# Feed-forward gate and up as 2x2 blocks with seven products instead of eight

## The chip, the cores and the metric

The kernel runs on one core of one Trainium2 chip. The metric is the device time of one execution in microseconds. Three runs of the kernel before took 2939.01, 2939.33 and 2942.37 us; the median is 2939.33 us.

## The reference, cut to what matters

Two transformer-like blocks are computed for 1024 tokens of width 1024, in float32. The change touches the end of the first block, its feed-forward part:

```
h2 = ada_norm(x, norm2_g, sh2, sc2)
gt, up = jnp.split(h2 @ w_gu, 2, axis=-1)          # w_gu: 1024 x 5632, D_FF = 2816
x = x + g2 * ((jax.nn.silu(gt) * up) @ w_down)     # w_down: 2816 x 1024
```

D_FF is 22 tiles of 128 features. A second block (a state-space mixer, then a stick-breaking attention) follows. Its modulation vectors come from three matrices `ada_w_2` and `kv_ada_w_2` times an activated vector `c_2`; that product has nothing to do with the feed-forward and is computed beside it.

## The kernel before, in words

Everything is kept transposed: 128 features on the partitions, 1024 tokens along the row. Every float32 factor is split into a high part, which ScalarE copies to the type fp32r, and a low part, which VectorE subtracts (raw minus high). A product is then three matmuls: high by high, high by low, low by high. A matmul has a 128x128 weight and 512 tokens. `hH` and `hL` are the high and low parts of the eight tiles of h2.

A gate or up tile is one unit: 8 input tiles, 2 token halves and 3 products, 48 matmuls, into one of two PSUM units `PU`. A panel of weights (`w_raw`, 512 KB; `split` on ScalarE and on VectorE) holds one unit's weights. SyncE loads the panels in the order of use. `w_raw`, `w_hi_t` and `w_lo_t` have two buffers each.

Tile 0 is special: its gate and up run on the un-normalised tiles while the norm is still being computed, and are scaled afterwards. VectorE meanwhile writes the normalised tiles (`row_scaled` writes a tile `n_h`, `row_low` writes its low part). Tile 1's gate and up (`paired`, L1158) start when the tiles come, one tile after another.

Then ten rounds of a loop (`ffn_body`) follow, each for two tiles: gate, up, gate, then `down` of the two tiles before, then up. `down` takes two gated tiles as input: 2 panels of 4 units with 12 matmuls each; VectorE adds every unit to the residual `xT` (L3283). The gated tiles never leave the chip. ScalarE computes silu of the gate (L2372), VectorE multiplies by up (L3274), and both split the product (L2377, L3278).

In the first eight rounds a job runs beside: eight slabs of 128x1024 of the modulation matrices, loaded by GpSimd (L975, L977), multiplied and accumulated by VectorE (L2765), transposed and reduced (L2754, L2755) and turned into a column by four narrow matmuls on TensorE (`ada_columns`, L1204), which wait for the reduction (`ada_acc_s`). A slab is loaded when the slab two before it is used (`ada_used`).

Each engine executes its own list in the order written; waits are semaphores.

Of the kernel before, what the change touches and what calls it, by code (L numbers as in the profile page):

```python
# [166 lines left out]
M_UNIT0 = len(WIN_UNITS) + HEAD_UNITS + TT // 2 + KD + 4 * (FT // 2) + KD * (FT // 2)  # L167
# [22 lines left out]
OUT_PANEL0 = len(WIN_UNITS) + KD + 6 * (FT // 2) + 14 * NG + 2 * KD + 2 * SB_PAIRS  # L190
# [36 lines left out]
RAW_SCALED = 5  # L227
W_OUT_ORDER = (0, 1, 2, 3, 4, 6, 7, 5)
# [3 lines left out]
def two_blocks(nc, a, out):  # L232
# [8 lines left out]
    scr_g = nc.dram_tensor("mixer_inverse_rows", (KD, TT, 2, P), F32, kind="Internal").ap()  # L241
    scr_y = [nc.dram_tensor(f"kept_group_{n}", (4, P, T), F32, kind="Internal").ap() for n in ("high", "low")]
    ctx = ExitStack()
    with ctx:
# [105 lines left out]
        f_silu = at("f_silu", A, [P, 2, T])  # L350
        f_prod = at("f_prod", A + 2048, [P, 2, T])
        f_hi = at("f_hi", A + 4096, [P, 2, T], F32R)
        f_lo = at("f_lo", A + 6144, [P, 2, T], F32R)
# [6 lines left out]
        dt_p = at("dt_p", A + 13312, [P, KD, NH])  # L360
# [109 lines left out]
        ada0_landed = [sem(f"ada0_landed{n}") for n in range(4)]  # L470
# [12 lines left out]
        x_landed = [sem(f"x_pair_landed{t}") for t in range(TT // 2)]  # L483
# [22 lines left out]
        nv_tr = sem("na_values_transposed")  # L506
        nv_tok = sem("na_values_token_major")
        na_s = sem("na_scores_done")
        na_l = sem("na_logits_ready")
        na_e = sem("na_exp_done")  # L510
        na_tr = sem("na_probs_transposed")
        na_ev = [sem("na_probs_evacuated_even"), sem("na_probs_evacuated_odd")]
        na_evx = sem("na_last_keys_evacuated")
        na_pv = sem("na_values_summed")
        na_o = sem("na_output_written")
        wu_landed = sem("w_uq_w_ukv_landed")
        q_rot = sem("mla_queries_rotated")
        kr_landed = sem("mla_rotary_keys_placed")
# [3 lines left out]
        mla_m = sem("mla_minimum_ready")  # L522
# [81 lines left out]

        block = ctx.enter_context(nc.Block())
# [3 lines left out]
        def _(sp):  # L609
# [69 lines left out]
            def gate_up(i, t, up):  # L679
                panel(w_gu[:, :, bass.ds((2 * i + t) * P + up * DFF, P)], KD, P)  # L680
# [13 lines left out]
            for t, up in ((0, 0), (0, 1), (1, 0), (1, 1)):  # L694
                if (t, up) == (1, 0):
                    token_rows(0)
                    sp.wait_ge(c_inv, INVERSES + 1)
                gate_up(0, t, up)
            with sp.Fori(0, FT // 2 - 1) as i:
                pc.enter(i, 6)  # L700
                gate_up(i + 1, 0, 0)
                gate_up(i + 1, 0, 1)
                gate_up(i + 1, 1, 0)
                down(i)
                gate_up(i + 1, 1, 1)
            pc.leave(FT // 2 - 1)
            down(FT // 2 - 1)


# [144 lines left out]
        def _(g):  # L854
# [94 lines left out]
            ada2 = a["ada_w_2"].rearrange("l (k p) c -> p l k c", p=P)  # L949
            kva = a["kv_ada_w_2"].rearrange("(k p) c -> p k c", p=P)  # L950
# [21 lines left out]
            with counted(g, 8, [(pc, KD), (slab, KD)]) as i:  # L972
                for k in range(KD):
                    sl = slab_free()
                    g.dma_start(ada_w[:, sl, 0:768].rearrange("p (l c) -> p l c", l=2), ada2[:, :, k, bass.ds(3 * P * i, 3 * P)])\  # L975
                        .then_inc(ada_landed[sl], 16)
                    g.dma_start(ada_w[:, sl, 768:1024], kva[:, k, bass.ds(2 * P * i, 2 * P)]).then_inc(ada_landed[sl], 16)  # L977
                    slab_next()
# [67 lines left out]
        def _(pe):  # L1046
# [21 lines left out]
            def feat_unit(wp, c0, width, kt, aH, aL, panel_last=True, mid=None, ready=None, late=None):  # L1068
# [3 lines left out]
                for half in range(2):  # L1072
                    cols = slice(half * 512, (half + 1) * 512)
                    for k in range(kt):
# [3 lines left out]
                        whi = w_hi_t[:, wp, w0:w0 + width]  # L1078
                        wlo = w_lo_t[:, wp, w0:w0 + width]
# [116 lines left out]
            def ada_columns():  # L1196

                n = job.next()
                s = (job.n - 1) % 2
                pe.wait_ge(ada_acc_s, n)  # L1200
                if job.n > 2:
                    pe.wait_ge(ada_mod, n - 2)
                for q in range(4):
                    last = mm(PM[32 * q:32 * q + 32, 2 + s, 0:KD], fold[:, 0:32], ada_red[:, s, q::4], start=True, stop=True)  # L1204
                last.then_inc(ada_col, 1)
# [363 lines left out]
            paired(hr())  # L1569
            hr.next(KD)  # L1570
            fa = Tally()

            def down():
                pe.wait_ge(f_act, fa.next(2))
                for c in range(2):
                    wp = panel_ready()
                    for u in range(4):
                        feat_unit(wp, u * P, P, 2, f_hi, f_lo, panel_last=u == 3)

            def last_down():  # L1580
                both = fa.next(2)
                wp, u0 = panel_ready(), unit_open()
                p1, n1 = uc.at(1)
                pair = ((u0, 0), (p1, P))

                def part(up, c0, k, half, w, side, first=False, final=False):
                    w0 = k * 512 + c0
                    return mm(PU[:, up, half, :], w[:, wp, w0:w0 + P], side[:, k, half * 512:(half + 1) * 512],
                              start=first, stop=final)

# [2177 lines left out]
```

## Time and profile before

| | |
|---|---|
| median of three runs | 2939.33 us |
| profiled execution, device time | 2943.62 us |
| its span | 2941.8 us |
| TensorE busy | 2870.7 us, 98% |
| VectorE busy | 1748.7 us, 59% |
| ScalarE busy | 1039.3 us, 35% |
| GpSimd busy | 446.6 us, 15% |
| mean granted TensorE clock | 0.991 |
| feed-forward, tile 0's gate to the last down unit | about 739 to 1465 us of the span |

Busy time of TensorE is counted from overlapping matmuls: one of 512 columns is shown as 0.39 us long, and the next starts 0.227 us after it. The distance between starts, not the length, says what a matmul costs.

### The profile page before, as it was taken

The page shows a single profiled execution, that of the slowest core. Times are in us where ns is not written, and L with a number is a line of the kernel's source. Part 1 is how long each engine was busy: PE and PEld are TensorE (multiplying, and loading weights), DVE is VectorE, ACT ScalarE, POOL GpSimd, SP SyncE. Part 2 cuts the span into 40 slices and gives each one's busy share as a digit, 9 for nine tenths or more (in the row PEclk, how much of TensorE's full clock was granted, in tenths as well). Part 3 has the DMA queues.
Part 4 walks back from the last instruction along what each step waited for, and adds up shares of the span by engine and source line. Part 5 has one row for each costly group of instructions (what it writes and reads, how often), then busy time and mean ns, then how long its engine had stood idle before and what let it go on. Part 6 is the DMA issues. An engine that isn't in the chain of part 4 may idle for free.

```text
span 2941.8 us, 40297 instructions
## 1 busy us (share of the span) xinstructions
PE 2870.7 (98%) x16452; PEld 2271.7 (77%) x16452; DVE 1748.7 (59%) x1932; ACT 1039.3 (35%) x1343; POOL 446.6 (15%) x508
## 2 busy tenths in 40 slices
PE   6998999999999999999999999999999999999999
PEld 5886667778888888888877888888778887777677
DVE  6557638763755555543467848668768345455463
ACT  4124445652411111111235424334434114444462
POOL 3012010001211111110102103021212002223240
PEclk8999999999999999999989999999999999999999
DMA  7454011101333333331115233243531321212121
GB/s 244 144 166 108 6 30 31 30 23 43 103 120 108 100 107 110 111 93 50 43 45 152 72 93 108 79 131 103 179 111 51 108 91 60 72 37 70 39 87 58
DMA packets 248122, 258.66 MB, mean 88 GB/s; under 512 B 14431, under 2 KB 208656, under 8 KB 247968
## 3 DMA queue, kind: packets, MB, share of 16 engines
q1 hardware_dynamic: 223280, 179.70, 19.9%
q0 software_dynamic: 19008, 59.19, 6.9%
q10 hardware_dynamic: 5680, 17.58, 1.5%
q8 instruction: 113, 1.85, 0.3%
q14 instruction: 41, 0.34, 0.0%
HBM read 223.41 MB, written 30.65 MB: 86 GB/s over the span
## 4 chain that ended last, share of the span: by engine, by line
PE 89%; DVE 4%; ACT 3%; issue 1%; DMA 1%; SPq 1%; POOL 0%; ACTq 0%; DVEq 0%; POOLq 0%
PE PU L1080 18%; PE PU L1082 17%; PE PU L1081 17%; PE PU L1858 2%; PE PM L1882 2%; PE PM L1870 2%; PE PM L1902 2%; PE PU L1096 2%; PE PU L1097 2%; PE PU L1098 2%; PE PU L1469 2%; PE PM L1904 2%; PE PM L1903 2%; PE PU L1391 2%; ACT m_p L2311 1%
## 5 line engine op out<-in xcount | busy, mean ns | idle before, releaser
L1080 PE MATMUL PU<-hH,w_hi_t 128*128 128x512 f32 x1792 | 706.1, 394 | 0.8 <-DVE w_lo_t L2727 0.6
L1082 PE MATMUL PU<-hH,w_lo_t 128*128 128x512 f32 x1792 | 698.4, 390 | 0.0
L1081 PE MATMUL PU<-hL,w_hi_t 128*128 128x512 f32 x1792 | 697.7, 389 | 0.0
L1082 PEld LDWEIGHTS PU<-hH,w_lo_t 128*128 128x128 f32 x1792 | 335.1, 187 | 72.4
L1080 PEld LDWEIGHTS PU<-hH,w_hi_t 128*128 128x128 f32 x1792 | 335.3, 187 | 71.5 <-issue 1.7
L1081 PEld LDWEIGHTS PU<-hL,w_hi_t 128*128 128x128 f32 x1792 | 335.4, 187 | 68.9
L2727 DVE TENSOR_TENSOR w_lo_t<-w_raw,w_hi_t 128x1024 fp32r<-128x1024 f32 x180 | 234.7, 1304 | 216.2 <-ACT w_hi_t L2016 208.4
L2016 ACT ACTIVATE w_hi_t<-w_raw 128x1024 fp32r<-128x1024 f32 x166 | 174.2, 1049 | 410.5 <-PE PU L1082 327.9
L3283 DVE SCALAR_TENSOR_TENSOR xT<-PU,mod,xT 128x1024 f32<-128x1024 f32 x120 | 153.8, 1282 | 158.5 <-PE PU L1082 158.5
L3627 DVE TENSOR_TENSOR_SCAN s_keep<-s_keep,zero 128x128 f32<-128x128 f32 (+7 forms) x128 | 182.0, 1423 | 76.3 <-POOL s_keep L1035 76.3
L1035 POOL TENSOR_SCALAR_AFFINE_SELECT s_keep<-s_keep 128x128 f32<-128x128 f32 x128 | 93.9, 740 | 467.0 <-ACT s_keep L2613 466.6
L1080 PE MATMUL PU<-f_hi,w_hi_t 128*128 128x512 f32 x344 | 133.9, 389 | 1.3 <-DVE xT L3283 1.3
L1082 PE MATMUL PU<-f_hi,w_lo_t 128*128 128x512 f32 x344 | 133.8, 389 | 0.0
L1081 PE MATMUL PU<-f_lo,w_hi_t 128*128 128x512 f32 x344 | 133.8, 389 | 0.0
L2620 ACT ACTIVATE s_at<-PM 128x128 f32<-128x128 f32 (+7 forms) x128 | 83.5, 652 | 141.7 <-PE PM L1870 141.2
L1096 PE MATMUL PU<-hH,w_hi_t 128*128 128x512 f32 x304 | 123.2, 405 | 6.3 <-DVE hL L2805 5.8
L1097 PE MATMUL PU<-hL,w_hi_t 128*128 128x512 f32 x304 | 120.5, 396 | 0.0
L1098 PE MATMUL PU<-hH,w_lo_t 128*128 128x512 f32 x304 | 120.2, 395 | 0.0
L998 POOL TENSOR_TENSOR xw<-xt,wend 128x512 f32<-128x512 f32 x28 | 38.0, 1357 | 499.3 <-PE PU L1082 195.7
L975 POOL DMA_DIRECT2D ada_w<-in_ada_w_dram x64 | 45.6, 713 | 433.7 <-DVE ada_acc L2765 305.0
L2765 DVE SCALAR_TENSOR_TENSOR ada_acc<-ada_w,cact,ada_acc 128x1024 f32<-128x1024 f32 x84 | 107.5, 1280 | 2.2
L1902 PE MATMUL PM<-hH,w_hi_t 128*128 128x512 f32 x224 | 98.7, 440 | 0.0
(518 smaller groups left out, 5007.5 us busy)
## 6 DMA issues: line engine op xcount, KB each, us to landing
ada_w<-in_ada_w_dram POOLq DMA_DIRECT2D x64, 384.0 KB, 4.0
w_raw<-in_w_gu_dram SPq DMA_DIRECT2D x44, 512.0 KB, 3.8
w_raw<-in_m_in_w_dram SPq DMA_DIRECT2D x40, 512.0 KB, 3.9
ada_w<-in_w_ada_dram POOLq DMA_DIRECT2D x32, 512.0 KB, 4.8
seg<-decay_sums SPq DMA_DIRECT2D x32, 512.0 KB, 4.1
w_raw<-in_w_down_dram SPq DMA_DIRECT2D x22, 512.0 KB, 3.3
w_raw<-in_w_in_dram SPq DMA_DIRECT2D x17, 512.0 KB, 3.9
ada_w<-in_w_ada_dram SPq DMA_DIRECT2D x16, 512.0 KB, 14.5
```

The source lines that it names most:

```text
L1080: mm(PU[0:width, up, half, :], whi, aH[:, k, cols], start=k == 0, stop=False)
L1081: mm(PU[0:width, up, half, :], whi, aL[:, k, cols], start=False, stop=False)
L1082: last = mm(PU[0:width, up, half, :], wlo, aH[:, k, cols], start=False, stop=k == kt - 1)
L1096: mm(PU[0:width, up, half, :], whi, hH[:, k, cols], start=first, stop=False)
L1097: mm(PU[0:width, up, half, :], whi, hL[:, k, cols], start=False, stop=False)
L1098: return mm(PU[0:width, up, half, :], wlo, hH[:, k, cols], start=False, stop=final)
L1902: mm(PM[:, 3, :], whi, hH[:, j, cols], start=j == 0, stop=False)
L2016: af(w_hi_t[:, p, 0:w], w_raw[:, p, 0:w], ACT.Copy).then_inc(w_hi[p], 1)
L2727: V.tensor_tensor(w_lo_t[:, p, 0:w], w_raw[:, p, 0:w], w_hi_t[:, p, 0:w].bitcast(F32), ALU.subtract)\
L2765: ins = V.scalar_tensor_tensor(acc, w, cv[:, k:k + 1], acc, ALU.mult, ALU.add)
L3283: free(V.scalar_tensor_tensor(xT[:, t, :], unit_ps(p), m(g, t), xT[:, t, :], ALU.mult, ALU.add))
L3627: V.tensor_tensor_scan(keep[:, ::-1], keep[:, ::-1], zero[:, :].broadcast_to([P, w]), 1.0, ALU.mult, ALU.max).then_inc(s_a, 1)
```

## The change

Tiles 2 to 21 (20 tiles) are computed as a 2x2 by 2x2 block product. The weight's four blocks are gate or up, by even or odd input tiles (each 4 tiles of 128x128). The input's four blocks are even or odd input tiles, by first or second 512 tokens. Eight block products become seven, each over 4 tiles: 7 x 4 x 3 = 84 matmuls for a tile's gate and up. A block product is a `phase`. The sums of input blocks are formed once by GpSimd from `n_h` (`t_formed`), and split by ScalarE and VectorE into `t_hi`, `t_lo` and the second half of the even tiles of `hH`, `hL`. The sums of weight blocks are formed for every tile by GpSimd (`weight_sums`, 4 operations of 128x512). Each phase's weight is split anew (`phase_high` on ScalarE, `phase_low` on VectorE, 128x512, four buffers). The results are combined in PSUM and by five VectorE additions.

The feed-forward becomes two passes. The first writes all gated tiles to DRAM (`scr_f`), the second loads them back and runs all eleven `down` pairs one after another, with the same 1056 matmuls as before. The modulation job is cut into 16 half jobs, one for each of the tiles 2 to 17, of 8 slabs of 128x512, now loaded by SyncE in two transfers each; `ada_columns` runs at the end of each of the 16 tiles.

SyncE, one body for four tiles (`rows_body`; `gate_up_rows` loads 2 x 512 KB, the weights of the tile after next):

```diff
+            def ada_slabs(i, r, ks):
+                c, l = 2 * i + r // 2, r % 2
+                for k in ks:
+                    if k == 1:
+                        sp.wait_ge(ada_acc_s, ADA_JOBS + 4 * i + r)
+                    else:
+                        sp.wait_ge(ada_used, slab(-1))
+                    dst = ada_half[:, k % 2, :]
+                    sp.dma_start(dst[:, 0:384], ada2[:, l, k, bass.ds(3 * P * c, 3 * P)]).then_inc(half_landed[k % 2], 16)
+                    sp.dma_start(dst[:, 384:512], kva[:, k, bass.ds(2 * P * c + l * P, P)]).then_inc(half_landed[k % 2], 16)
+                    slab.next()
+            def rows_body(i, jobs, rows=range(4)):
+                for r in range(4):
+                    if jobs:
+                        ada_slabs(i, r, range(4))
+                    if r in rows:
+                        sp.wait_ge(gu_low, GU_LOW + 28 * i + 7 * r + 7)
+                        gate_up_rows(r, 4 * i + r + 4)
+                    if jobs:
+                        ada_slabs(i, r, range(4, KD))
...
+            gate_up_rows(0, 2)
+            sp.wait_ge(unit_free[1], D_UNIT0 // 2)
+            sp.dma_start(scr_f[1, :, :], f_second[:, :]).then_inc(f_stored, 16)
+            sp.wait_ge(f_stored, F_STORED + 32)
+            gate_up_rows(1, 3)
```

TensorE:

```diff
+            def phase(i, r, q):
+                slot = phase_slot(7 * r + q)
+                pe.wait_ge(gu_low, GU_LOW + 28 * i + 7 * r + q + 1)
...
+                for k in range(4):
...
+                    mm(bank, gu_hi[slot][:, k, :], high, start=first, stop=False, skip_group_check=check)
+                    mm(bank, gu_hi[slot][:, k, :], low, start=False, stop=False, skip_group_check=check)
+                    last = mm(bank, gu_lo[slot][:, k, :], high, start=False, stop=k == 3, skip_group_check=check)
+                last.then_inc(gu_done, 1)
+            def phases_body(i, jobs):
+                for r in range(4):
+                    for q in range(7):
+                        phase(i, r, q)
+                    if jobs:
+                        ada_columns(4, half_columns)
+            with counted(pe, 4, [(job, 4)]) as i:
+                phases_body(i, 1)
+            phases_body(4, 0)
```

VectorE, for one tile r (`tt` is an addition; `done` counts the tile's finished phases):

```diff
+                    phase_low(i, r, 4)
+                    half_slabs((0, 1))
+                    ve.wait_ge(gu_done, done + 2)
+                    tt(mid, PM[:, 1, :], mid, ALU.add).then_inc(gu_added, 1)
+                    phase_low(i, r, 5)
+                    ve.wait_ge(gu_done, done + 3)
+                    ve.wait_ge(f_kept, F_KEPT + 64 * i + 16 * r)
+                    tt(f2, PM[:, 2, :], mid, ALU.add).then_inc(gu_added, 1)
+                    phase_low(i, r, 6)
+                    half_slabs((2, 3))
+                    ve.wait_ge(gu_done, done + 4)
+                    tt(f2, PM[:, 3, :], f2, ALU.add).then_inc(gu_added, 1)
...
+                        phase_low(i, r + 1, 0)
+                        half_slabs((4, 5))
+                        phase_low(i, r + 1, 1)
+                        half_slabs((6, 7))
...
+                    ve.wait_ge(gu_done, done + 6)
+                    tt(f1, PM[:, 2, :], mid, ALU.add).then_inc(gu_added, 1)
+                        phase_low(i, r + 1, 2)
+                    ve.wait_ge(gu_done, done + 7)
+                    tt(mid, PM[:, 3, :], mid, ALU.add).then_inc(gu_added, 1)
+                        phase_low(i, r + 1, 3)
```

GpSimd, and the waits that its sums put into VectorE's norm loop; and VectorE in the second pass:

```diff
+            for k in range(4):
+                g.wait_ge(h_tmp, KD + 2 * k + 2)
...   # four subtractions of 128x512, each counted by t_formed
+            def halves_gated(i, r):   # two multiplications of 128x512, then the store
...
+                g.dma_start(scr_f[bass.ds(4 * i + r + 2, 1), :, :].rearrange("o p t -> (o p) t"), f_out[:, :]).then_inc(f_kept, 16)
...
+                    if k:
+                        ve.wait_ge(t_formed, T_FORMED + (4 * (k // 2) + 2 if k % 2 else 2 * k))
                     row_scaled(k + 1, coef[:, 1, :], n_rs[:, :])
...
+            def down_body(b):
+                down_units("g2", range(4))
+                tile_low(2 * b)
+                tile_low(2 * b + 1)
+                down_units("g2", range(4, 8))
```

`phase_high` on ScalarE waits until the phase four before it is done (`gu_done`). `gate_up_rows(0, 2)` waits for all sixteen input sums. At the end of the first pass ScalarE waits for the last store (`f_kept`) before it splits the second down panel.

## Rows read from the trace of the kernel before

**Rows 1.** The page: engines, and the chain that ended last.
```profile
PE 2870.7 (98%) x16452; PEld 2271.7 (77%) x16452; DVE 1748.7 (59%) x1932; ACT 1039.3 (35%) x1343; POOL 446.6 (15%) x508
PE 89%; DVE 4%; ACT 3%; issue 1%; DMA 1%; SPq 1%; POOL 0%; ACTq 0%; DVEq 0%; POOLq 0%
```

**Rows 2.** Windows: busy PE, PEld, DVE, ACT, POOL; clock; DMA share; GB/s.
```profile
881.00:944.00 63.00, 63.00 (x286) 51.91 (x285) 34.04 (x31) 10.08 (x10) 8.46 (x14) 1.00 0.35 105
```

**Rows 3.** Timeline of TensorE: start, length, line, tiles.
```profile
1000.24 0.39 PE L1080 MATMUL PU<-hH,w_hi_t 128*128 128x512 f32 x1
...
1005.68 0.39 PE L1080 MATMUL PU<-hH,w_hi_t 128*128 128x512 f32 x1
```

**Rows 4.** Timeline of VectorE in the loop.
```profile
897.60 1.28 DVE L3283 SCALAR_TENSOR_TENSOR xT<-PU,mod,xT 128x1024 f32<-128x1024 f32 x1 [0.30 <-PE PU L1082]
900.32 1.28 DVE L3283 SCALAR_TENSOR_TENSOR xT<-PU,mod,xT 128x1024 f32<-128x1024 f32 x1 [1.44 <-PE PU L1082]
...
911.86 1.25 DVE L2754 STREAM_TRANSPOSE ada_acc<-ada_acc 128x1024 f32<-128x1024 f32 x1
913.14 1.22 DVE L2755 TENSOR_REDUCE ada_red<-ada_acc 128x32 f32<-128x1024 f32 x1
...
977.56 1.25 DVE L2754 STREAM_TRANSPOSE ada_acc<-ada_acc 128x1024 f32<-128x1024 f32 x1
```

**Rows 5.** Groups by shape, VectorE and ScalarE: count, busy, mean ns.
```profile
L3442 DVE TENSOR_TENSOR xt<-xt,xl 128x512 f32<-128x512 f32 x28 | 19.4, 692 | 1.0
L3429 DVE TENSOR_TENSOR state<-state,PM 128x512 f32<-128x512 f32 x24 | 16.5, 687 | 0.8
L3158 DVE SCALAR_TENSOR_TENSOR y_att<-y_att,vec,PM 128x512 f32<-128x512 f32 x2 | 1.5, 747 | 3.9 <-PE PM L1519 3.9
L2298 ACT ACTIVATE m_pt<-PM 128x512 f32<-128x512 f32 x64 | 34.8, 594 | 81.3 <-PE PM L1483 81.2
```

**Rows 6.** Tile w_raw, its issues (ns min/median/max); transfers in 1334:1342.
```profile
L628 SPq DMA_DIRECT2D w_raw<-in_w_gu_dram x5: 372/373/373, 1335.6 to 1400.9; - x5
w_raw<-in_w_gu_dram SPq DMA_DIRECT2D x1, 512.0 KB, 3.7
q1 hardware_dynamic: 1040, 0.52, 22.3%
```

**Rows 7.** Timeline of GpSimd and VectorE, alone and side by side.
```profile
719.77 2.40 POOL L960 TENSOR_TENSOR n_acc<-n_acc,n_sq 128x1024 f32<-128x1024 f32 x1 [8.48 <-ACT n_sq L2044]
741.53 3.34 POOL L960 TENSOR_TENSOR n_acc<-n_acc,n_sq 128x1024 f32<-128x1024 f32 x1 [1.87 <-ACT n_sq L2044]
730.68 6.72 DVE L2820 SCALAR_TENSOR_TENSOR hL<-xT,coef,hH 128x1024 fp32r<-128x1024 f32 x5
741.34 5.81 DVE L2820 SCALAR_TENSOR_TENSOR hL<-xT,coef,hH 128x1024 fp32r<-128x1024 f32 x3
```

**Rows 8.** TensorE around a pause: windows of 1 us, and its timeline.
```profile
424.00:425.00 1.00, 1.00 (x14) 0.77 0.07 16
425.00:426.00 1.00, 1.00 (x8) 0.50 0.00 0
420.38 1.84 PE L1507 MATMUL PM<-blk,u_sq 128*128 128x2 f32 x16
423.64 0.50 PE L1461 MATMUL PU<-kr_hi,w_lo_t 32*128 32x512 f32 x4 [1.41 <-ACT m_p L2311]
425.55 0.63 PE L1469 MATMUL PU<-k_hi,qk_lo 64*128 64x512 f32 x2
```

**Rows 9.** Timeline, VectorE's norm loop and tile 1's results.
```profile
755.24 1.29 DVE L2805 SCALAR_TENSOR_TENSOR hL<-n_h,mod,hH 128x1024 fp32r<-128x1024 f32 x1
773.75 2.59 DVE L2805 SCALAR_TENSOR_TENSOR hL<-n_h,mod,hH 128x1024 fp32r<-128x1024 f32 x2
785.66 1.23 DVE L3274 TENSOR_TENSOR f_prod<-PU,f_silu 128x1024 f32<-128x1024 f32 x1 [0.85 <-PE PU L1098]
```

**Rows 10.** Timeline of TensorE at the end of the feed-forward.
```profile
1448.75 0.50 PE L1080 MATMUL PU<-f_hi,w_hi_t 128*128 128x512 f32 x1 [1.28 <-DVE xT L3283]
```

More of the change, by code:

```diff
@@ L710, in _ @@
+            with sp.Fori(0, 4) as x:
+                pc.enter(x, 4)
+                for b in range(2):
+                    down_body(2 * x + 1 + b, b)
+                pc.leave(4)
+            down_body(9, 0)
+            down(10)
             m_in = a["m_in_w_2"].rearrange("o (k p) c -> p (o k) c", p=P)
@@ L971, in _ @@
                     g.dma_start(small[32 * q:32 * q + NH, c:c + 1], a[name].rearrange("o h -> h o")).then_inc(rp_landed, 16)
[L972 to L978, printed above, removed]
+            even, odd = n_h[:, 0, :], n_h[:, 1, :]
@@ L2365, in _ @@
-            up = Tally(1)
-            def gate(t, ahead=False):
-                if not ahead:
-                    split()
-                p = unit()
-                free(af(f_silu[:, t, :], unit_ps(p), ACT.Silu))
-            def high(t, upu):
-                act.wait_ge(unit_free[upu[0]], upu[1] + 1)
-                up.next()
-                af(f_hi[:, t, :], f_prod[:, t, :], ACT.Copy).then_inc(f_hi_s, 1)
+            af(f_first[:, 0, :], f_first[:, 0, :], ACT.Silu, bias=small[:, 44:45]).then_inc(raw_gate, 1)
@@ new lines, in _ @@
+            for n in range(2):
+                for k in range(4):
+                    token_sum_high(n, k)
+            act.wait_ge(raw_scaled, 4)
+            phase_high(0, 0, 0)
+            token_sum_high(3, 0)
+            token_sum_high(3, 1)
+            act.wait_ge(f_stored, F_STORED + 16)
+            phase_high(0, 0, 1)
+            token_sum_high(3, 2)
+            p = unit()
+            free(af(f_second[:, :], unit_ps(p), ACT.Silu))
+            token_sum_high(3, 3)
+            used.next(KD - 1)
@@ L2379, in passed @@
+            with act.Fori(0, 4) as i:
+                highs_body(i)
+            highs_body(4, last=True)
+            for n in (2, 3):
+                tile_high(n, 1)
             def passed(units):
@@ L3298, in ffn_body @@
+            with counted(ve, 4, [(slab, 4 * KD), (job, 4), (reduced, 4), (ch, 4)]) as i:
+                lows_body(i, 1)
+            lows_body(4, 0, last=True)
+            tile_low(2)
+            tile_low(3)
+            ve.wait_ge(gu_done, GU_DONE + 7 * F_PAIRS)
+            down_units("g2", range(4))
+            down_units("g2", range(4, 8))
+            def down_body(b):
                 down_units("g2", range(4))
+                tile_low(2 * b)
+                tile_low(2 * b + 1)
                 down_units("g2", range(4, 8))
-                low(0)
@@ L3301, in ffn_body @@
-                up(1, todo[6:8])
-                low(1)
-                if jobs:
-                    ada_finish([(48 + 3 * i, 128 + 3 * i, 3), (72 + 3 * i, 152 + 3 * i, 3), (96 + 2 * i, 176 + 2 * i, 2)])
-                for c in (pc, uc, fh, job, slab, ch):
-                    c.leave(times)
-            low(0)
-            gate(ahead=True)
-            up(1)
-            low(1)
-            with ve.Fori(0, 8) as i:
-                ffn_body(i, 8, 1)
-            with ve.Fori(0, FT // 2 - 9) as i:
-                ffn_body(i, FT // 2 - 9, 0)
+            with counted(ve, 4, [(pc, 4), (uc, 16), (fh, 4)]):
+                down_body(0)
+                down_body(1)
```

476 lines of the change are left out of this document (313 added, 163 removed).

## The prediction

> **What bounds the kernel now.** I read the page first: TensorE is busy for 98% of the span and holds 89% of the chain that ended last [rows 1]. The window of one round of the feed-forward loop shows the same locally: TensorE busy for 63.00 of 63 us at full clock, VectorE for 34.04, GpSimd for 8.46, DMA share 0.35 [rows 2]. The busy sum can't price a matmul, because they overlap. In the timeline 24 matmuls start between 1000.24 and 1005.68 [rows 3], so one of 512 columns costs 0.227 us. A round has 4 x 48 + 8 x 12 = 288 matmuls, 65.3 us; two transposes of the job one round apart lie 65.7 us apart [rows 4]. The 0.4 us left are the narrow `ada_columns`. So TensorE alone sets the loop, and nothing else waits on its path.
>
> **What the change removes.** A tile's gate and up go from 96 to 84 matmuls, 21.8 to 19.0 us; a phase is 12 matmuls, 2.72 us. With 20 tiles that is 54.4 us. The `ada_columns` run 16 times instead of 8, 3.4 us more. If TensorE stayed the bound, 51 us would be gained. The 1056 `down` matmuls stay.
>
> **What it adds to a tile with a job (16 of the 20).** VectorE: 7 lows at 0.69 (two SBUF inputs), 5 additions from PSUM at 0.69, 8 half slabs at 0.75, a transpose and a reduction at about 0.7 each (half of 1.25 and 1.22 plus a start-up part) [rows 4, 5]: 15.6 us of 19.5. GpSimd: 6 operations of 128x512; one of 1024 takes 2.40 alone [rows 7], so about 1.2 each, and a store's issue: 8 us. ScalarE: 7 highs, a copy and two silus at 0.6 [rows 5], 6 us. DMA: 1 MB of weights, 2 MB of slabs, 0.5 MB stored. A 512 KB panel used 0.223 of 8 us [rows 6], 1.8 us of all engines, so 12 us. Every engine has room for its sum. So the order has to be walked, because TensorE ends each such tile with `ada_columns`, which waits for the reduction of this same tile's job.
>
> I count from the start of the tile's first phase. The third phase ends at 8.2 (3 x 2.72). Only then may ScalarE make the high part of the seventh phase (four buffers), and VectorE has the addition of the third phase before its low part: 0.7 and 0.7, with a little delay by GpSimd 10.0. SyncE has waited for just this low part, with the slabs 4 to 7 queued behind the wait. It issues the 2 x 512 KB of weights at 10.1. One panel lands 3.7 us after its issue [rows 6], the second 1.8 later: 15.6. Slab 4 (256 KB, 0.9 of data) stands behind them: 16.5. No row of before shows a small transfer behind two panels; the ends are 13.7 (issued 0.8 later, since an issue takes 0.37 [rows 6], landing 2.8, no queue) and 16.5, and I take the upper, since both lie on one queue that is full for those 3.6 us. Slab 4 is used by 17.3. Only that lets SyncE issue slab 6, which lands 2.8 later (3.7 less half the data), 20.2 with the hand-overs. Slabs 6 and 7 take VectorE to 21.7, transpose and reduction to 23.1, the columns to 23.6. TensorE finished its seven phases at 19.0 and stands idle for 4.1 us.
>
> The Trainium skill bears on the choice between the two ends (DMA: Bandwidth & Descriptors, Queues, rings and completion order): SyncE's transfers share one row of rings, and on each DMA engine descriptors are consumed in ring order. By that rule slab 4 waits for both panels and the tile takes 23.6 us; without it 20.8. No row here shows it.
>
> The pause has a second price. After 1.84 us of two-column matmuls and 1.41 us idle the granted clock fell to 0.50, and 512-column matmuls grew to 0.63 us [rows 8], for about 3 us. That is at most 1.6 us lost, part of it in the pause itself or behind the third phase, where it is covered. Between 0 and 1.6 I take 0.6. A tile with a job: 24.2 us against 21.97 before (half of 65.7 less 21.76 of `down`). 16 x 2.2 = +35.7 us.
>
> The other four tiles have no slabs. VectorE needs 8.3 of 19.0 us there and each low part is ready two phases early; 4 x (19.04 - 21.76) = -10.9.
>
> **Contention.** GpSimd and VectorE slow each other: `hL` takes 6.72 / 5 = 1.34 us alone, but three take 5.81 while GpSimd's addition runs, and that one grows from 2.40 to 3.34 [rows 7]. A 1024 operation on GpSimd costs VectorE up to 1.8 us, a 512 one 0.9; six make 5.4 at worst. Most fall where VectorE waits anyway; 0.3 us stands in the 10.0 above, up to 2 in the upper bound.
>
> **The start.** Four subtractions per pair of tiles, 4.8 us alone, now stand between `n_h` pairs: with one `row_scaled` (1.28) 6.1 us a pair, 8 with contention, against 5.1 before. The loop ran from 755.2 to 776.3 and tile 1's units ended at 785.6, without waiting for it [rows 9]; they had about 2 us of slack at the fourth tile. So tile 1 is late by 0 to 4 us. The first weight rows are loaded only after the last sum (781 to 787), take 5.5 to land and 1.4 to split: the first phase starts 2 to 8 us late. In its first tile SyncE stores tile 1, waits for that (about 3 us) and loads the next rows before any slab: the reduction comes 3 to 12 us later than in the steady walk. Together 5 to 20; I take +12.
>
> **Middle and second pass.** After the last phase: addition, silu, product, store and its landing, about 7 us, then the split of the second down panel. VectorE has that split ahead of its first evacuation, so the third unit waits: +4 (0 to 6). In each later pair two low parts and a split stand between evacuations 4 and 5: 10.9 + 1.3 + 3 x 1.2 + 1.3 = 17.1, while unit 7 wants its PSUM at 16.3 (units 2.72 us apart [rows 4]); overlapping starts take some back: 0.5 x 10 = +5 (0 to 8). The wait of 1.28 before the last `down` goes [rows 10]: -1.3.
>
> **Sum.** 35.7 - 10.9 + 12 + 4 + 5 - 1.3 = +44.5 us. The profiled execution took 2943.6 (span 2941.8 and 1.8 around it), so 2988 on its own time; the median is 4.3 lower, so 2984.
>
> **The rivals.**
> TensorE stays the bound (faster). If the reduction comes within 19.0 us, `ada_columns` finds it ready, and the tile costs 19.46: 16 x (19.46 - 21.97) = -40.2; -10.9; start +6, middle +4, second pass +5, -1.3: -37, 2902 us. For it: every engine has 20% to spare, and in the job before the reduction lay far ahead. It decides at the low part of the seventh phase plus 9 us; against it are the two serial landings with a panel pair in front of them.
> The slabs don't queue behind the panels. Slab 4 is there at 13.7, and all behind it is 2.8 us earlier: tile 20.8, 16 x -1.17 = -18.7; -10.9, start +8, +7.7 for the rest: -14, 2925 us. For it: the data are 0.9 us and the engines many. From a tile of 21.7 us on it is no gain.
> The pause feeds itself (slower still). The half clock hits the first phases in full, +1.6, and contention delays the seventh low part by 1.3: tile 26.5, 16 x 4.5 = +72; -10.9, start +18, rest +12: +91, 3030 us. For it are rows 7 and 8; against it, that a clock back at full inside 3 us leaves most of it covered.
>
> **How the numbers follow.** My walk 0.58, TensorE bound 0.14, no queue 0.14, feeding pause 0.14. The likeliest gives 2984 us; its own range is 2955 to 3012 (tile of 23 to 25.2, start 5 to 20). The range for 8 in 10 leaves out TensorE bound and the far part of the feeding pause: 2922 to 3020. A change of 0.2%, 6 us, is about what a measurement of this kernel can tell from none. Faster: 0.14 + 0.10 (most of no queue) = 0.24. Same: 0.05 (the edge of no queue and of my walk). Slower: 0.71.
>
> **What would show it.** In the profile after, two `ada_columns` of neighbouring tiles lie about 24 us apart in tiles 2 to 17 and 19 in the last four. In the first 16 TensorE waits about 4 us for VectorE's reduction, once a tile, and the clock shows 0.50 right after. The transfers of slab 4 land 6 us after the panel pair is issued. The second pass has waits of under 1 us for an evacuation. What would make me wrong: `ada_columns` without a wait before it, slabs landing in 3 us with panels in flight, or waits in front of the phases themselves, which the walk says have at least 5 us in hand.

## The result, and the profile after

The changed kernel took 3065.54 us (median of four runs, 3061.1 to 3070.56), the kernel before 2940.85 us beside it. The ratio is 1.0421, with a 95% interval of 1.0408 to 1.0434. It is slower, as forecast, but by 124.7 us where I forecast 45, and outside my range of 2922 to 3020. The profiled execution took 3061.1 us, the lowest of the four. Its span is 3059.5 us, 117.7 more than before, and the account below is of those 117.7.

First the page after: engines, and the chain that ended last. TensorE has less work than before, but its share of the chain fell from 89% [rows 1] to 74%, and a wait for slabs of the job (`ada_half`) stands in it.

```profile
PE 2865.9 (94%) x16276; PEld 2255.6 (74%) x16276; DVE 1928.4 (63%) x2217; ACT 1109.3 (36%) x1499; POOL 592.1 (19%) x536
PE 74%; DVE 9%; DMA 5%; issue 4%; ACT 4%; SPq 2%; POOL 1%; ACTq 0%; DVEq 0%; POOLq 0%
```

The windows show where: the fifteen tiles with a job behind the first (845 to 1249), the four without, and the second pass. Columns as in [rows 2]: the stretch, its length, busy PE, PEld, DVE, ACT, POOL, granted clock, DMA share, GB/s.

```profile
845.00:1249.00 404.00, 322.98 (x1372) 260.12 (x1370) 264.31 (x360) 90.47 (x150) 146.10 (x105) 0.88 0.45 136
1249.00:1329.00 80.00, 78.59 (x344) 64.57 (x344) 40.32 (x53) 24.55 (x39) 34.25 (x25) 0.97 0.28 92
1329.00:1583.00 254.00, 244.78 (x1056) 198.47 (x1056) 161.19 (x137) 51.20 (x50) 14.76 (x7) 0.99 0.25 87
```

In the first stretch TensorE is idle for a fifth of the time and its clock is 0.88, against 63.00 of 63 and 1.00 in [rows 2]. A tile takes 27.0 us there (the first and the last of sixteen reductions start at 843.20 and 1248.37, 15 tiles). No engine but TensorE is over 66% busy. The list of waits names one wait for all of it: line, what it waited for, us in total, times, longest.

```profile
PE PU L1357 <- DVE ada_red L2954: 87.3, 16, 7.1
```

One tile in detail, from TensorE's timeline. The columns wait for the reduction, as forecast, for 5 us. The first phase behind them starts its matmuls 0.427 us apart instead of 0.227 [rows 3]; it takes 5.3 us (1060.38 to 1065.67) instead of 2.72.

```profile
1060.16 0.29 PE L1357 MATMUL PU<-ada_red,fold 128*32 128x4 f32 x8 [4.99 <-DVE ada_red L2954]
1060.38 0.80 PE L1744 MATMUL PM<-hH,gu_hi 128*128 128x512 f32 x1
1060.98 0.63 PE L1745 MATMUL PM<-hL,gu_hi 128*128 128x512 f32 x1
1061.40 0.63 PE L1746 MATMUL PM<-hH,gu_lo 128*128 128x512 f32 x1
...
1065.67 0.41 PE L1744 MATMUL PM<-t_hi,gu_hi 128*128 128x512 f32 x1
```

Windows of 1 us, TensorE alone (busy, clock, DMA share, GB/s), show why: the clock is at 0.50, the lower level of 1.2 GHz, from 1059 to 1065.65. TensorE had been idle since about 1055.2.

```profile
1058.00:1059.00 1.00, 0.00 (x0) 0.94 0.43 115
1059.00:1060.00 1.00, 0.00 (x0) 0.50 0.48 147
...
1064.00:1065.00 1.00, 1.00 (x4) 0.50 0.00 0
1065.00:1066.00 1.00, 1.00 (x5) 0.65 0.12 49
```

The job's chain in the same tile: VectorE's timeline (the seventh low part, slabs 4 and 5, 6, 7, the reduction), then SyncE's (the panel pair, slab 4, slab 6).

```profile
1072.51 0.68 DVE L3486 TENSOR_TENSOR gu_lo<-gu_sum,gu_hi 128x512 fp32r<-128x512 f32 x1
...
1080.18 1.54 DVE L2964 SCALAR_TENSOR_TENSOR ada_half_acc<-ada_half,cact,ada_half_acc 128x512 f32<-128x512 f32 x2 [3.42 <-DMA ada_half<-in_kv_ada_w_dram]
...
1083.74 0.75 DVE L2964 SCALAR_TENSOR_TENSOR ada_half_acc<-ada_half,cact,ada_half_acc 128x512 f32<-128x512 f32 x1 [1.41 <-DMA ada_half<-in_kv_ada_w_dram]
1084.99 0.75 DVE L2964 SCALAR_TENSOR_TENSOR ada_half_acc<-ada_half,cact,ada_half_acc 128x512 f32<-128x512 f32 x1 [0.50 <-DMA ada_half<-in_kv_ada_w_dram]
...
1086.52 0.69 DVE L2954 TENSOR_REDUCE ada_red<-ada_half 128x16 f32<-128x512 f32 x1
```

```profile
1073.37 1.01 SPq L749 DMA_DIRECT2D gu_rows<-in_w_gu_dram  x2
1074.63 0.75 SPq L764 DMA_DIRECT2D ada_half<-in_ada_w_dram  x1
...
1081.10 0.33 SPq L764 DMA_DIRECT2D ada_half<-in_ada_w_dram  x1
```

Counted from the first phase at 1060.38, with the forecast in brackets: the panels are issued at 13.0 (10.1), slab 4 is used from 19.8 (landed at 16.5), slab 6 from 23.4 (20.2), the reduction ends at 26.8 (23.1). The order of events is that of the walk in the prediction. Of the 3.7 us that it is late, 2.9 are there when the panels are issued, and 2.6 of these are the slow first phase.

The start, from VectorE's and GpSimd's timelines. Beside GpSimd's subtractions VectorE's operations on 128x1024 take 2.29 instead of 1.29 us, and GpSimd's on 128x512 take 2.24 instead of 1.31: both take 1.7 to 1.8 times as long.

```profile
754.42 1.29 DVE L3005 SCALAR_TENSOR_TENSOR hL<-n_h,mod,hH 128x1024 fp32r<-128x1024 f32 x1
...
762.85 2.29 DVE L3005 SCALAR_TENSOR_TENSOR hL<-n_h,mod,hH 128x1024 fp32r<-128x1024 f32 x1
```

```profile
758.04 1.31 POOL L1086 TENSOR_TENSOR t_raw<-n_h 128x512 f32<-128x512 f32 x1
...
766.60 2.24 POOL L1086 TENSOR_TENSOR t_raw<-n_h 128x512 f32<-128x512 f32 x1 [2.55 <-DVE n_h L3001]
```

The loop over the normalised tiles takes 39.2 us (751.90 to 791.1), against 23.6 before (752.7 to 776.3 [rows 9]). TensorE's first phase starts at 806.69:

```profile
806.69 0.79 PE L1744 MATMUL PM<-hH,gu_hi 128*128 128x512 f32 x1 [7.83 <-DVE gu_lo L3486]
```

The second pass, from VectorE's timeline: two low parts and a split stand before an evacuation, and a pair of gated tiles is 22.59 us from the next (1369.06 to 1391.65) instead of 8 x 2.72 = 21.76 [rows 4].

```profile
1369.06 2.35 DVE L3510 TENSOR_TENSOR f_lo<-f_raw,f_hi 128x1024 fp32r<-128x1024 f32 x2
1371.33 1.22 DVE L2926 TENSOR_TENSOR w_lo_t<-w_raw,w_hi_t 128x1024 fp32r<-128x1024 f32 x1
1372.46 2.47 DVE L3461 SCALAR_TENSOR_TENSOR xT<-PU,mod,xT 128x1024 f32<-128x1024 f32 x2
...
1391.65 2.35 DVE L3510 TENSOR_TENSOR f_lo<-f_raw,f_hi 128x1024 fp32r<-128x1024 f32 x2
```

The account of the 117.7 us beside that of the prediction:

| part | forecast | measured | how measured |
|---|---|---|---|
| 16 tiles with a job | +35.7 | +80.6 | 16 x (27.0 - 21.97) |
| 4 tiles without | -10.9 | -7.2 | 1249.4 to 1329.2, less 4 x 21.76 |
| start | +12 | +32.2 | first phase 806.7, not 784.8 (785.6 [rows 9] less 0.8): 21.9; first tile 37.3, not 27.0: 10.3 |
| middle and second pass | +9 | +14.4 | 1329.2 to 1583.0, less 11 x 21.76 |
| wait before the last `down` | -1.3 | -1.3 | gone |
| loop starts earlier | 0 | -0.8 | 751.9, not 752.7 |
| sum | +44.5 | +117.9 | |

### The profile page after: what moved, and what is told of

It reads as the page before. It is cut to its first block, busy times and chain, and to the rows that moved or that the text cites. A ratio compares the mean times of both kernels' runs of the same rounds, so it can differ in the third digit from the quotient of the medians.

```text
span 3059.5 us, 41804 instructions
## 1 busy us (share of the span) xinstructions
PE 2865.9 (94%) x16276; PEld 2255.6 (74%) x16276; DVE 1928.4 (63%) x2217; ACT 1109.3 (36%) x1499; POOL 592.1 (19%) x536
## 4 chain that ended last, share of the span: by engine, by line
PE 74%; DVE 9%; DMA 5%; issue 4%; ACT 4%; SPq 2%; POOL 1%; ACTq 0%; DVEq 0%; POOLq 0%
PE PU L1232 12%; PE PU L1234 11%; PE PU L1233 11%; DMA ada_half<-in_kv_ada_w_dram 4%; PE PU L1998 2%; PE PM L2022 2%; PE PM L2010 2%; PE PM L2042 2%; PE PM L1744 2%; PE PM L2044 2%; PE PM L2043 2%; PE PU L1622 2%; PE PU L1248 2%; PE PM L1745 2%; PE PM L1746 2%
## 5 line engine op out<-in xcount | busy, mean ns | idle before, releaser
L1232 PE MATMUL PU<-hH,w_hi_t 128*128 128x512 f32 (+1 forms) x1152 | 455.9, 396 | 0.7 <-DVE w_lo_t L2926 0.6
L1234 PE MATMUL PU<-hH,w_lo_t 128*128 128x512 f32 (+1 forms) x1152 | 449.2, 390 | 0.0
L1233 PE MATMUL PU<-hL,w_hi_t 128*128 128x512 f32 (+1 forms) x1152 | 448.7, 389 | 0.0
L1234 PEld LDWEIGHTS PU<-hH,w_lo_t 128*128 128x128 f32 (+1 forms) x1152 | 214.9, 187 | 47.2
L1232 PEld LDWEIGHTS PU<-hH,w_hi_t 128*128 128x128 f32 (+1 forms) x1152 | 215.2, 187 | 46.4 <-issue 1.5
L1233 PEld LDWEIGHTS PU<-hL,w_hi_t 128*128 128x128 f32 (+1 forms) x1152 | 215.3, 187 | 44.0
L1744 PE MATMUL PM<-hH,gu_hi 128*128 128x512 f32 x320 | 142.0, 444 | 14.4 <-DVE gu_lo L3486 7.8
L1248 PE MATMUL PU<-hH,w_hi_t 128*128 128x512 f32 x304 | 125.1, 411 | 15.8 <-DVE hL L3005 8.4
L1745 PE MATMUL PM<-hL,gu_hi 128*128 128x512 f32 x320 | 137.8, 431 | 0.0
L1249 PE MATMUL PU<-hL,w_hi_t 128*128 128x512 f32 x304 | 121.7, 400 | 0.0
```

The lines of the kernel that those rows point to most:

```text
L1232: mm(PU[0:width, up, half, :], whi, aH[:, k, cols], start=k == 0, stop=False)
L1233: mm(PU[0:width, up, half, :], whi, aL[:, k, cols], start=False, stop=False)
L1234: last = mm(PU[0:width, up, half, :], wlo, aH[:, k, cols], start=False, stop=k == kt - 1)
L1248: mm(PU[0:width, up, half, :], whi, hH[:, k, cols], start=first, stop=False)
L1249: mm(PU[0:width, up, half, :], whi, hL[:, k, cols], start=False, stop=False)
L1744: mm(bank, gu_hi[slot][:, k, :], high, start=first, stop=False, skip_group_check=check)
```

## The experiments

The kernels are all built from the changed one ("after", 3065.5 us). A tile means the mean distance of the sixteen reductions.

**The slabs first.** The queue behind the panels is taken away. SyncE loads all eight half slabs of a tile before it waits for the seventh low part:

```diff
                     if jobs:
-                        ada_slabs(i, r, range(4))
+                        ada_slabs(i, r, range(KD))
                     if r in rows:
                         sp.wait_ge(gu_low, GU_LOW + 28 * i + 7 * r + 7)
                         gate_up_rows(r, 4 * i + r + 4)
-                    if jobs:
-                        ada_slabs(i, r, range(4, KD))
```

> The load order of SyncE alone is changed: all eight half slabs of a tile are issued before SyncE waits for the seventh low part and loads the next pair of weight panels. After, a tile with a job takes 27.0 us; slab 4 lands about 7 us after the panel pair's issue, and the reduction ends 15.9 us behind the third phase. Theory A (the two serial slab landings behind the panel pair set the tile): slab 4 no longer waits for the seventh low part or for the panels, the reduction comes 4 to 6 us earlier, TensorE's pause shrinks from 5 us to 0 to 1.5, and with it the time at half clock: tile 20.5 to 22.5 us, 16 x (-4.5 to -6.5) = -72 to -104 us, 2960 to 2995 us. Theory B (VectorE's slab work and its contention with GpSimd set the reduction, the landing is hidden behind them): the reduction moves by under 1.5 us, tile 25.5 to 27 us, 3040 to 3066 us. Theory C (panels now late behind the slabs): the waits move to the first phase of the next tile, tile above 24 us with TensorE waiting for a low part at the head of a tile, 3015 us or more.

Measured: 3009.22 us, 56 less than after, ratio 1.0229 to before (1.0212 to 1.0246); tile 23.7 us. That is between the theories. VectorE's timeline of this kernel (slabs 5, 6 and 7, the reduction), and SyncE's issues of the same three slabs:

```profile
950.70 0.75 DVE L2962 SCALAR_TENSOR_TENSOR ada_half_acc<-ada_half,cact,ada_half_acc 128x512 f32<-128x512 f32 x1 [0.91 <-DMA ada_half<-in_kv_ada_w_dram]
952.58 0.75 DVE L2962 SCALAR_TENSOR_TENSOR ada_half_acc<-ada_half,cact,ada_half_acc 128x512 f32<-128x512 f32 x1 [0.53 <-DMA ada_half<-in_kv_ada_w_dram]
954.39 0.75 DVE L2962 SCALAR_TENSOR_TENSOR ada_half_acc<-ada_half,cact,ada_half_acc 128x512 f32<-128x512 f32 x1 [1.05 <-DMA ada_half<-in_kv_ada_w_dram]
...
955.92 0.69 DVE L2952 TENSOR_REDUCE ada_red<-ada_half 128x16 f32<-128x512 f32 x1
```

```profile
948.04 0.33 SPq L764 DMA_DIRECT2D ada_half<-in_ada_w_dram  x1
...
949.95 0.33 SPq L764 DMA_DIRECT2D ada_half<-in_ada_w_dram  x1
...
951.61 0.33 SPq L764 DMA_DIRECT2D ada_half<-in_ada_w_dram  x1
```

From issue to use a slab takes 2.6 to 2.8 us with no panel ahead of it. In after slab 4 took 5.55 (1074.63 to 1080.18). The difference, 2.9 us, is what the 1 MB of panels ahead of it costs per tile, and the tile fell by 3.3. The Trainium skill (DMA: Bandwidth & Descriptors, Queues, rings and completion order) says that on each DMA engine descriptors are consumed in ring order, and these two numbers agree with it. They don't tell an order in the queue from panels and slab merely sharing the DMA engines; no run here separates the two. I had expected more because I overlooked that slabs 2 to 7 still stand behind the seventh low part in VectorE's own order, and then come one every 1.85 us, the turn-round of two buffers.

**The columns later.** The consumer is moved: `ada_columns` and VectorE's copy of them go behind the second phase of the next tile.

```diff
                     for q in range(7):
                         phase(i, r, q)
-                    if jobs:
-                        ada_columns(4, half_columns)
+                        if q == 1 and r in tiles:
+                            ada_columns(4, half_columns)
```

> Only the place of the consumer is changed: TensorE runs the four small column products of a tile's job behind the second phase of the next tile (VectorE's copy of them moves with it), loads and slab work stay in their order. If the 7.6 us by which a tile with a job exceeds its 84 matmuls and its columns (27.0 against 19.45) are all a wait for the reduction plus the half clock behind this wait, then 5.4 us of slack take the wait away whole, the clock stays up and the tile falls to 19.5 to 21.0 us: 16 x (-6 to -7.5) = -96 to -120, 2945 to 2970 us. If the job's chain itself is longer than a tile (the slabs and the low parts on VectorE and SyncE take over 21 us per tile whatever the place of the columns), the waits come back at the phases: tile 22 to 25 us, 2985 to 3035 us, with TensorE waiting for a low part.

Measured: 3024.82 us, ratio 1.0284 (1.0267 to 1.0301), tile 24.6 us. The second case. Two phases of slack took away only 2.4 us. VectorE's timeline (reduction, an addition, the low part of the next tile's third phase) and TensorE's show it:

```profile
1015.96 0.69 DVE L2955 TENSOR_REDUCE ada_red<-ada_half 128x16 f32<-128x512 f32 x1
1016.56 0.68 DVE L3560 TENSOR_TENSOR f_out<-PM,gu_mid 128x512 f32<-128x512 f32 x1
1017.16 0.68 DVE L3487 TENSOR_TENSOR gu_lo<-gu_rows,gu_hi 128x512 fp32r<-128x512 f32 x1
```

```profile
1016.77 0.25 PE L1357 MATMUL PU<-ada_red,fold 128*32 128x4 f32 x8 [2.10 <-DVE ada_red L2955]
...
1017.97 0.49 PE L1744 MATMUL PM<-t_hi,gu_hi 128*128 128x512 f32 x1 [0.95 <-DVE gu_lo L3487]
```

The third phase waits as well. So the tile is set by a ring, a chain of waits that closes on itself: the reduction stands ahead of the third phase's low part in VectorE's list; the third phase ahead of the seventh low part; this ahead of the panels; these ahead of slab 4; and slab 4 ahead of the next reduction.

**The pause filled.** This aims at the clock alone: 18 matmuls whose result is thrown away stand where TensorE was idle.

```diff
                     if jobs:
+                        for _ in range(18):
+                            mm(PU[:, 0, 1, :], hH[:, 1, 0:P], hH[:, 1, 0:512], start=True, stop=True)
                         ada_columns(4, half_columns)
```

> 18 matmuls of 128x512 whose product nobody reads (4.1 us at full clock) are put before the column products of each tile with a job, where TensorE stands idle for 5 us; nothing else is changed. They take nothing from the chain that ends in the reduction. If the half clock in the next tile's first phase (5.3 us instead of 2.72) is a cost of the pause and on the path, the clock stays at or near full and the tile falls from 27.0 to 24.3 to 24.9 us: -34 to -43 us, 3022 to 3032 us, and what remains is the walk's 23.6 us plus about 1. Rival, as the prediction had it: the half clock is mostly covered, the tile falls by 0.6 or less (3056 to 3066 us); or the extra matmuls run late and push the columns: 3066 us or more.

Measured: 3053.18 us, 12 less, ratio 1.0379 (1.0362 to 1.0396), tile 26.4 us on average. Neither expectation holds for the mean. Where the clock stayed at 1.00 a tile is 25.4 to 25.9 us; the others are 26.7 to 28.1. Windows of single tiles (columns as above):

```profile
898.00:926.00 28.00, 26.00 (x110) 20.99 (x110) 17.76 (x25) 6.03 (x10) 9.71 (x7) 0.89 0.45 133
1057.00:1082.00 25.00, 23.61 (x110) 19.24 (x110) 17.85 (x24) 6.04 (x10) 9.79 (x7) 1.00 0.49 142
```

The fill doesn't close the pause: 2.0 us of idle time are left before the columns at 1083.15, and 3.9 before those at 899.17, and the phase behind the latter runs at half clock (the tile of the first row). At full clock the tile gives back 1.4 of the 2.6 us; the tiles of after all lie between 26.7 and 27.6. The rest goes to hand-overs (what passes between the end of one step and the start of the next): with the phases earlier, the sixth low part meets a GpSimd sum (1.18 us instead of 0.68), and the panels are asked for 3.1 us behind the third phase instead of 2.2. So where the clock stays up it is worth 1.4 us a tile, more than twice what I took, though over all sixteen tiles the fill gave only 0.65. In the run with the slabs first the tiles part in the same way: 23.7 to 23.9 us where the clock is 0.93, and 22.5 and 22.8 in the two where it stayed up (a window of each kind):

```profile
932.00:956.00 24.00, 21.15 (x92) 17.02 (x92) 18.37 (x26) 6.03 (x10) 9.79 (x7) 0.93 0.52 156
1026.00:1049.00 23.00, 19.53 (x92) 15.85 (x92) 18.63 (x25) 6.37 (x11) 9.82 (x7) 1.00 0.56 166
```

The run with the columns later shows the opposite: its tiles take 24.3 to 25.1 us whether their clock is 1.00, 0.93 or 0.86, so there the slow matmuls are covered. In the filled run one tile at a clock of 0.99 (871 to 898) still took 27.6 us, since slab 4 came 8.4 us behind the panels' issue there instead of 6.7; why, is open.

**No jobs.** The sixteen modulation jobs are left out on all engines (TensorE's part is shown), and their 64 columns of the modulation set to 0.

```diff
-            with counted(pe, 4, [(job, 4)]) as i:
-                phases_body(i, 1)
+            with pe.Fori(0, 4) as i:
+                phases_body(i, 0)
```

> The sixteen modulation jobs inside the feed-forward are left out: no slabs, no slab work, no reduction, no column products (their 64 output columns of the modulation are set to 0, part of the computation that is not done). It isolates everything else that the change adds. If the jobs' chain is the whole loss, the sixteen tiles run like the last four, at 19.1 to 19.9 us: 16 x -7.4 = -118, less 3 to 8 at the first tile: 2935 to 2950 us, so about at the time of before, which still does its jobs; the first pass itself then costs what its matmuls cost. If contention, the stores or the reload of the rows bind also without jobs, the tiles stay over 21 us: 2975 us or more.

Measured: 2925.16 us, ratio 0.9937 (0.992 to 0.9953). The tiles then run at TensorE's pace, 19.2 us each (the twenty lie between 807.3 and 1191), and 140 us of after are the jobs. That is 10 us below the range expected: each tile gave back 7.8 us, not 7.4, and the first one its whole extra of 10.3. Even without its jobs the kernel, with its start and second pass as they are, gains only 18 us on the one before, which has them in.

**Both.** Slabs first and columns later in one kernel.

> The two edits together: slabs issued ahead of the panels, and the column products behind the second phase of the next tile. With the columns moved alone the tile stayed at 24.6 us: the pause at the columns shrank, but the tile is now set by a ring that closes on VectorE: the reduction stands in front of the low part of the next tile's third phase, that phase in front of the seventh low part, this in front of the panels, these in front of slab 4 and so of the next reduction. Ring theory: moving the slabs ahead of the panels takes 2.9 us out of this ring, as it did alone (27.0 to 23.7, of which 0.4 was clock): tile 21.4 to 22.0, 2975 to 2990 us. Rival (no ring; the two edits take away the whole wait): tile 19.5 to 20.3, 2940 to 2958 us.

Measured: 2973.76 us, ratio 1.011 (1.0094 to 1.0125), tile 21.6 us. The ring forecast this, not its rival: 24.6 less 2.9 is 21.7.

**The ring cut.** As both, and VectorE takes the slabs from 2 on one at a time. The last slab, the transpose and the reduction now stand behind the first four low parts of the next tile; before, the reduction stood ahead of the third.

```diff
                     phase_low(i, r, 5)
+                    half_slabs((2,))
...
                     phase_low(i, r, 6)
-                    half_slabs((2, 3))
+                    half_slabs((3,))
...
                         phase_low(i, r + 1, 0)
-                        half_slabs((4, 5))
+                        half_slabs((4,))
                         phase_low(i, r + 1, 1)
-                        half_slabs((6, 7))
+                        half_slabs((5,))
...
                         phase_low(i, r + 1, 2)
+                        half_slabs((6,))
...
                         phase_low(i, r + 1, 3)
+                        half_slabs((7,))
```

> As the two edits together, and VectorE uses the half slabs one at a time between the low parts and additions of a tile, with the last one, the transpose and the reduction behind all low parts of the next tile's first phases. Nothing that TensorE's phases need then stands behind a slab that may be late, and the reduction has two phases of slack before its columns. Ring theory: the ring is cut, tile 19.5 to 20.3 us, 16 x (-6.7 to -7.5) against the 27.0 of after: 2945 to 2960 us. Rival (VectorE's sum binds: 18 us of work a tile, stretched by GpSimd): the tile is 20.5 to 21.5 us and TensorE waits for low parts all over the tile: 2962 to 2980 us.

Measured: 2945.9 us (ten runs), ratio 1.0011 (1.0002 to 1.0021), tile 20.0 us, 19.5 to 19.9 in the last eight. The ring was the cause: the three edits bring 120 us back without a single operation less. The spreading was run only together with the other two.

**The small loads and the second pass.** Added to this: GpSimd's ten small loads behind its subtractions, and the low parts of the second pass one by one between evacuations.

```diff
-                down_units("g2", range(4))
+                down_units("g2", range(2))
                 tile_low(2 * b)
+                evacuated("g2", 2)
                 tile_low(2 * b + 1)
+                evacuated("g2", 3)
```

> The former, with GpSimd's ten small loads behind its sixteen subtractions instead of ahead of them, and the two low parts of a pair of gated tiles in the second pass put between the evacuations 2 and 3 and 3 and 4, not both together with the split between 4 and 5. The loads: they take GpSimd from 752.5 to 758.0 before its first subtraction, so the first phase starts 3 to 6 us earlier. The low parts: a pair of tiles costs TensorE 22.6 us against 21.76, so -5 to -9 us over the ten pairs. Together -8 to -15 against the former: 2932 to 2950 us, within 0.4% of before. If the late evacuation is not due to the low parts, the second pass stays at 253.8 us; if the loop over the normalised tiles is paced by GpSimd's sums alone, the start gains under 2 us.

Measured: 2937.46 us (eleven runs), ratio 0.9981 (0.9972 to 0.999). Two splits one pair apart in the second pass lie exactly 21.76 us apart:

```profile
1307.35 1.22 DVE L2926 TENSOR_TENSOR w_lo_t<-w_raw,w_hi_t 128x1024 fp32r<-128x1024 f32 x1
...
1329.11 1.22 DVE L2926 TENSOR_TENSOR w_lo_t<-w_raw,w_hi_t 128x1024 fp32r<-128x1024 f32 x1
```

From the last reduction to the last evacuation it is 319.1 us, against 328.0 with the ring cut alone; these 8.9 us are the whole gain on that kernel (8.4 between the medians). The loop over the normalised tiles is 36.7 us (752.87 to 789.5), 2.5 less. But the 3 to 6 us expected from the loads did not come: the first phase starts at 806.57, 53.7 us behind the loop's start, against 54.8 both in after and with the ring cut (753.40 to 808.21).

```profile
806.57 0.80 PE L1743 MATMUL PM<-hH,gu_hi 128*128 128x512 f32 x1 [10.54 <-DVE gu_lo L3486]
```

There the rival came true: the start gained under 2 us.

**Fills for subtractions.** Built from after: GpSimd writes a constant instead of each of the sums, which are not computed (one of the four lines is shown).

```diff
-                nc.gpsimd.tensor_tensor(t1, even[:, b2_], even[:, b1], ALU.subtract).then_inc(t_formed, 1)
+                nc.gpsimd.memset(t1, 0.5).then_inc(t_formed, 1)
```

> GpSimd's sixteen subtractions of the token sums are replaced by fills of the same 512 columns with a constant, so the sums of the tokens are not computed; everything else is as after. It separates what GpSimd's reading costs: in after, the loop over the normalised tiles takes 39 us (751.9 to 791.1) against 23.6 before, VectorE's 1024-column operations in it take 2.29 us against 1.28 alone, and GpSimd's 512-column ones 2.14 to 2.28 against 1.3. If this contention and the length of the subtractions are the cause: VectorE's operations are back at 1.28, the loop at 24 to 28 us, the whole 10 to 18 us shorter (3048 to 3056 us). Rival: GpSimd's small loads and ScalarE's pace set it, the loop stays over 33 us and the whole within 5 us of after.

Measured: 3049.87 us, 15.7 less than after, ratio 1.0365 (1.0346 to 1.0383). From the timelines of VectorE and GpSimd:

```profile
762.46 1.28 DVE L3005 SCALAR_TENSOR_TENSOR hL<-n_h,mod,hH 128x1024 fp32r<-128x1024 f32 x1
```

```profile
762.60 0.53 POOL L1086 MEMSET t_raw<- 128x512 f32 x1 [2.91 <-DVE n_h L3001]
```

VectorE's operations are back at 1.28 us, also beside a fill as here, and the loop takes 25.8 us. A fill is 0.8 us shorter than a lone subtraction as well, so this run takes away contention and length together; the next one keeps the work. The Trainium skill (GPSIMD Engine Reference, Specifications) says that GpSimd shares its SBUF interfaces with VectorE and contends with instructions that have two SBUF inputs. The rows of this loop agree, and put the price at about 1 us on an operation of either engine that meets a whole one of the other. In the job tiles VectorE's low parts of 128x512 grow by 0.5 us beside GpSimd (1.18 instead of 0.68).

**The subtractions on VectorE.** The same sixteen, in VectorE's list behind each pair of tiles, from after:

```diff
                 row_low(k, m("sh2", 0, 8))
+                if k % 2 == 0:
+                    token_sums(k // 2)
```

> As after, but the sixteen subtractions of the token sums run on VectorE, between its own steps of the loop over the normalised tiles, instead of on GpSimd beside it. Contention theory (with fills in place of GpSimd's subtractions VectorE's 1024-column operations were back at 1.28 us, the loop took 26 us instead of 39 and the whole was 15.7 us shorter): VectorE does 16 x 0.6 to 0.7 = about 10 us more work in the loop, but alone, so 8 x 2 x 1.2 + 2.4 + 10 = 31.6 to 33 us instead of 39.2, and the two products behind it are 2 to 3 us shorter: 6 to 9 us in all, 3056 to 3060 us. Rival (VectorE is the bound there either way, and the added 10 us cost as much as the contention did): within 3 us of after.

Measured: 3056.36 us, 9.2 less than after, ratio 1.0385 (1.0369 to 1.0401). The loop ends at 784.2, 32.2 us long: more work on the busier engine, and sooner done. Here is one of the moved operations, from VectorE's timeline:

```profile
763.80 0.69 DVE L3430 TENSOR_TENSOR t_raw<-n_h 128x512 f32<-128x512 f32 x1
```

**All six edits.** The subtractions are now on VectorE, so GpSimd's small loads no longer stand ahead of anything that the loop needs.

> The five edits so far and this one in one kernel. The former took 2937.5 us; of its 36.7 us loop 4 to 5 should go, and 2 to 3 behind it, if contention is the cause: 2928 to 2933 us, 0.3 to 0.5% faster than before. If VectorE's own sum binds there: 2935 to 2940 us.

Measured: 2927.48 us against 2943.17 beside it, ratio 0.9949 (0.9935 to 0.9962). This version beats both kernels, the one before by half a per cent. Its window over some fifteen job tiles (columns as above) is full, like [rows 2]:

```profile
845.00:1140.00 295.00, 293.82 (x1382) 237.31 (x1381) 241.28 (x355) 89.36 (x151) 142.45 (x105) 1.00 0.62 183
```

A tile takes 19.8 us. Of the 51 us that the smaller number of matmuls could give, 16 x (21.97 - 19.8) = 35 come from the job tiles, and the start still eats some 24: the first phase starts at 795.2 instead of 784.8, and the first reduction comes at 828.2, 13 us behind the steady pace.

## Why the prediction was wrong

**What held.** The mechanism: TensorE's last step of a tile waits for this tile's reduction, through two serial slab landings with the panels ahead of them, once in each of the sixteen tiles. The upper of my two ends for slab 4, queued behind the panels, was the right one: 2.9 us measured, 2.8 taken. The four tiles without a job, the late evacuation in the second pass (+0.83 a pair, 0.5 taken) and the middle were right within 6 us each. "TensorE stays the bound" is refuted by the wait that all sixteen tiles have, "the slabs don't queue" by the 2.9 us.

**Where it failed, first: the clock.** The step is "The pause has a second price ... Between 0 and 1.6 I take 0.6". From [rows 8] I read that half clock lasts about 3 us, and argued that part of it falls into the pause. The pause was 5 us, and the half clock lasted 6.7 us, through the whole first phase: 2.6 us longer. In the filled run the tiles that kept the full clock gave back 1.4 of this; how much of the rest is covered, no run shows. The walk itself turns on the third phase, so a slow first phase shifts every later step, the next pause included. The third rival said this, with 1.6 us, and I gave it 0.14. Its tile of 26.5 lies near the measured 27.0, but in part by luck: it had 1.3 us for contention at the seventh low part, where 0.3 more than in the walk was measured (panels issued 2.2 us behind the third phase, 1.9 in the walk).

**Second: the start,** +32 instead of +12. I took "8 with contention" a pair of tiles; the pairs are 10.6 us apart (760.63, 771.09, 781.82). I had the rate from [rows 7], where one GpSimd operation met three of VectorE's, and charged only VectorE with it. In this loop both engines are slowed at once and each waits for the other, so the two stretches add up in series. Fills in place of the subtractions took 15.7 us off. My first tile's extra of 3 to 12 us was right (10.3).

**Third: small hand-overs,** 0.8 us a tile between the panels' issue and the reduction (13.8 us against 13.0 in the walk). Over sixteen tiles that is 13 us.

Clock and hand-overs make 16 x 2.8 = 45 of the 73 us that the sum lacks, the start 20, the last four tiles and the second pass 9. Between the medians the change is another 7 us larger: the profiled execution was the fastest of its kernel, by 4.4 us, and the one before lay 2.8 above its median.

What stays open: why slab 4 lands up to 1.7 us later in some tiles, whether it waits for its turn behind the panels or shares the engines with them, and how the 6.7 us of half clock divide between the path and its cover.

## What to carry to other kernels

When every engine has room for its sum and the time still rises, write the waits down as a ring through the in-order lists, the loading engine's included, and ask which entry is there only by its place. Here three such places (slabs behind a wait, a consumer right behind its producer, low parts behind slabs) cost 120 us, and the two edits that I tried alone each gave back less than half of it. A pause that repeats in a loop should be priced up to the full length of the slow matmuls that follow it (2.6 us a tile here, of which 1.4 came back), and two engines that share a path should both be charged.

## What the runs showed of the hardware

TensorE, idle since 1055.2, was at a granted clock of 0.50 from about 1058.9 and stayed there for 6.7 us, 5.3 of them at full work. VectorE and GpSimd side by side on SBUF data: 1.28 grows to 2.29 us on VectorE (128x1024, two SBUF inputs), 1.3 to 2.2 us on GpSimd (128x512), while a fill of 128x512 on GpSimd takes 0.53 us and leaves VectorE at 1.28 (762.46, beside the fill at 762.60). Moving that work to the busier engine made the loop 7 us shorter. A 256 KB slab took 2.7 us from issue to use with a free queue, and 5.55 with 1 MB ahead of it.
